# Hybrid RWKV-7 / forgetting-attention / MoE layer on one core: the forget gate in five pieces, one sum of squares a unit later, and the norms' chains in other places of the order

## The reference

```python
# forget gate of the attention
log_f = jax.nn.log_sigmoid(fl + f_bias)              # fl: 8 columns of u
c = jnp.transpose(jnp.cumsum(log_f, axis=1), (0, 2, 1))
s = jnp.einsum('bqhd,bkhd->bhqk', qb, k) + cb[..., :, None] - c[..., None, :]
...
o = o * lax.rsqrt(jnp.mean(o * o, axis=-1, keepdims=True) + RMS_EPS)   # norm of each head
# RWKV: the normalised kk, and the norm of y
kk = kk / jnp.maximum(jnp.sqrt(jnp.sum(kk * kk, axis=-1, keepdims=True)), 1e-12)
mean = jnp.mean(y, axis=-1, keepdims=True)
var = jnp.mean(jnp.square(y - mean), axis=-1, keepdims=True)
y = ((y - mean) * lax.rsqrt(var + RWKV_GN_EPS)).reshape(B, T, RWKV_WIDTH) * ln_w + ln_b
bonus = jnp.sum(r * k * r_k, axis=-1, keepdims=True) * v
return (y + bonus.reshape(B, T, RWKV_WIDTH)) * g
```

## Time and profile before

| | |
|---|---|
| median of 3 runs | 1685.38 us (1681.61 to 1690.52) |
| the profiled execution, its own time | 1686.94 us |
| its span | 1685.1 us |
| TensorE busy | 1606.7 us (95%) |
| VectorE busy | 1333.5 us (79%) |
| ScalarE busy | 1029.3 us (61%) |
| GpSimd busy | 605.2 us (36%) |
| granted TensorE clock, mean | 0.977 of full speed |

### The profile page before, as it was taken

How to read it: one execution, slowest core, us unless ns; L and a number is a source line. 1 busy time by engine, 2 the same in 40 slices (tenths; PEclk the granted TensorE clock), 3 DMA queues, 4 the chain that set the end, 5 groups by cost and what they waited for, 6 DMA issues and landing times.

```text
span 1685.1 us, 23225 instructions
## 1 busy us (share of the span) xinstructions
PE 1606.7 (95%) x7860; PEld 1166.6 (69%) x7860; DVE 1333.5 (79%) x1172; ACT 1029.3 (61%) x890; POOL 605.2 (36%) x398
## 2 busy tenths in 40 slices
PE   6999999989998999999999999999999999999993
PEld 5677877878566767777777777777777777777772
DVE  4479765434268989999899998999989999989893
ACT  4345235322155767777777777777777777777772
POOL 5633520232343213334344334343343432334320
PEclk9999979999998999999999999999999999999997
DMA  5322110201249999999999999999999999999994
GB/s 175 97 76 73 37 15 1 101 1 51 64 181 370 324 385 373 381 376 373 373 380 381 375 378 360 381 383 372 380 377 371 380 380 374 380 367 383 382 344 132
DMA packets 146543, 467.08 MB, mean 277 GB/s; under 512 B 21015, under 2 KB 35005, under 8 KB 146429
## 3 DMA queue, kind: packets, MB, share of 16 engines
q1 hardware_dynamic: 136684, 437.36, 69.0%
q0 software_dynamic: 9664, 28.53, 7.2%
q10 hardware_dynamic: 144, 0.52, 0.1%
HBM read 443.67 MB, written 22.71 MB: 277 GB/s over the span
## 4 chain that ended last, share of the span: by engine, by line
PE 82%; DVE 7%; DMA 5%; issue 2%; ACT 2%; POOL 1%; SPq 0%; DVEq 0%; POOLq 0%; ACTq 0%
PE banks L1638 20%; PE banks L1640 20%; PE banks L1639 20%; PE banks L1583 2%; PE banks L1312 2%; PE banks L1313 2%; PE banks L1314 2%; DMA slots<-in_expert_w_dram 2%; PE banks L1647 2%; PE banks L1633 1%; PE banks L1667 1%; PE banks L1489 1%; PE banks L1479 1%; PE banks L1376 1%; PE banks L1508 1%
## 5 line engine op out<-in xcount | busy, mean ns | idle before, releaser
L1963 DVE TENSOR_TENSOR lo<-slots,hi 128x2048 fp32r<-128x2048 f32 x384 | 863.0, 2286 | 55.9 <-PE banks L1640 49.1
L1107 ACT CAST hi<-slots 128x2048 fp32r<-128x2048 f32 x384 | 734.0, 1912 | 246.4 <-PE banks L1640 139.2
L1638 PE MATMUL banks<-lo,x_hi 128*96 128x512 f32 x1024 | 407.6, 398 | 0.0
L1640 PE MATMUL banks<-hi,x_lo 128*96 128x512 f32 x1024 | 403.8, 394 | 0.0
L1639 PE MATMUL banks<-hi,x_hi 128*96 128x512 f32 x1024 | 402.7, 393 | 0.0
L903 POOL DMA_INDIRECT x_sum<-hT,idy x32 | 91.1, 2848 | 468.3 <-ACT hT L1190 454.5
L928 POOL COPY idx_all<-ovf_pair 96x2 int32 x28 | 160.8, 5744 | 156.8 <-DMA ovf_pair<-slot_tokens,ovf_col 156.8
L1640 PEld LDWEIGHTS banks<-hi,x_lo 128*96 128x96 f32 x1024 | 165.7, 162 | 72.0
L1639 PEld LDWEIGHTS banks<-hi,x_hi 128*96 128x96 f32 x1024 | 166.3, 162 | 67.6
L1638 PEld LDWEIGHTS banks<-lo,x_hi 128*96 128x96 f32 x1024 | 166.0, 162 | 66.8 <-issue 0.2
L1638 PE MATMUL banks<-lo,a_hi 128*96 128x512 f32 x512 | 202.9, 396 | 6.0 <-DVE a_lo L2146 4.1
(11 more groups left out here) (369 smaller groups left out, 1964.2 us busy)
## 6 DMA issues: line engine op xcount, KB each, us to landing
slots<-in_expert_w_dram SPq DMA_DIRECT2D x384, 1024.0 KB, 10.2
slots<-in_w_in_dram SPq DMA_DIRECT2D x13, 1024.0 KB, 5.2
xs<-in_x_dram SPq DMA_DIRECT2D x8, 512.0 KB, 5.8
slots<-in_w_out_dram SPq DMA_DIRECT2D x2, 2048.0 KB, 7.8
x_sum<-xs SPq DMA_DIRECT2D x4, 512.0 KB, 9.4
h_rows<-slots SPq DMA_DIRECT2D x4, 512.0 KB, 3.4
xs<-x_sum SPq DMA_DIRECT2D x4, 512.0 KB, 7.1
x_sum<-xs POOLq DMA_DIRECT2D x3, 512.0 KB, 10.3
```

The lines of the kernel that those rows point to most:

```text
L1107: nc.scalar.copy(w_hi[n % HI][:, :, :], raw[r]).then_inc(hi_ready, 1)
L1638: nc.tensor.matmul(out, x_h, w_l, start=first, stop=False)
L1640: return nc.tensor.matmul(out, x_l, w_h, start=False, stop=last)
L1963: tensor_tensor(w_lo[n % LO][:, :, :], raw[n % RAW], w_hi[n % HI][:, :, :], ALU.subtract).then_inc(lo_ready, 1)
```

## The change

1. **Forget gate in pieces.** The scratch rows `fz` move to another slot (free until later), DVE still takes `fz[0]` behind the mix of unit 0, but ACT makes Abs and Exp behind unit 1 and Ln behind unit 2, and DVE does the rest behind the mix of unit 4 (`FF_BEHIND`). ACT no longer waits for `c3_ready` before the sigmoids but before the exponentials behind unit 8.
2. **Sum of squares.** The last of the four (j = 3) moves on PE behind unit 16, its root on ACT behind unit 18, its taking on DVE to the second elementwise chain. Unit 16 and this sum swap their places in the rotation of banks.
3. **Attention's norm.** The root moves from step i % 8 == 1 to 2, the multiplication to 3, the transposes to 5; two steps are added at the end; the first scores stand behind the first two KAR stages instead of ahead of them.
4. **y's norm.** For chunks 0 and 1 the root (ACT) stands behind kt of the next chunk, the reciprocal (DVE) and POOL's six steps behind its first KAR stage. The place of yT on PE stays.

```diff
-        fz = [region(slot_flat[3], (4 + n) * T, T)[0:H, :] for n in range(3)]
+        fz = [region(slot_flat[2], (1 + n) * T, T)[0:H, :] for n in range(3)]
...
+        FF_BEHIND = 4
...
-                for j in range(JT):
+                for j in range(JT - 1):
                     rot(("ss", j))
+            if m == 16:
+                rot(("ss", JT - 1))
...
-        FOX_STEPS = len(units) + 4
+        FOX_STEPS = len(units) + 6
...
-        rwkv_stages = [fox_stages[0]] + [("KAR", 0, g, 0) for g in range(2)] + [fox_stages[1]] \
-            + [("KAR", 0, g, 1) for g in range(2)] + [fox_stages[2]] + [("BR", 0, g) for g in range(2)] \
-            + [fox_stages[3]] + [("vt", 0), ("bt", 0)]
+        rwkv_stages = [("KAR", 0, g, 0) for g in range(2)] + [fox_stages[0]] + [("KAR", 0, g, 1) for g in range(2)] \
+            + [fox_stages[1]] + [("BR", 0, g) for g in range(2)] + [fox_stages[2]] + [("vt", 0), ("bt", 0)] + [fox_stages[3]]
...
-                if kind == "yT":
...
+                if kind == "yT" and tt >= 2:
+                    scale_y(tt)
+                if st in (("KAR", 1, 0, 0), ("KAR", 2, 0, 0)):
+                    scale_y(tt - 1)
...
-                if m == 0:
-
+                if m == 1:
                     emptied(act, "ff")
                     step(nc.scalar.activation(fz[1], fz[0], ACT.Abs))
                     step(nc.scalar.activation(fz[1], fz[1], ACT.Exp, scale=-1.0))
+                if m == 2:
                     nc.scalar.activation(fz[1], fz[1], ACT.Ln, bias=1.0).then_inc(ffln_ready, 1)
                 if m == 3:
                     act.wait_ge(consts_ready, 3)
-                    act.wait_ge(c3_ready, 1)
...
+                    act.wait_ge(c3_ready, 1)
                     act.wait_ge(cum_ready, j + 1)
...
+                if m == 18:
+                    act.wait_ge(kksum_ready, JT)
+                    nc.scalar.activation(AR[:, JT - 1, :, 0:C], AR[:, JT - 1, :, 0:C], ACT.Sqrt).then_inc(kknorm_ready, 1)
...
-                if i > H and i % H == 1:
+                if i > H and i % H == 2:
                     fox_rms(act, i // H - 1)
-                if i > H and i % H == 3:
+                if i > H and i % H == 5:
                     fox_out_T(act, i // H - 1)
...
+                    if kind == "kt" and tt in (1, 2):
+                        y_deviation(tt - 1)
...
+                if m == 16:
+                    square_sums(JT - 1)
...
-                if i > H and i % H == 3:
+                if i > H and i % H == 5:
                     fo_transposes(i // H - 1)
...
+                if m == FF_BEHIND:
                     step(tensor_scalar(fz[2], fz[0], 0.0, None, ALU.min))
                     dve.wait_ge(ffln_ready, 1)
...
+                if j == 1:
+                    take_squares(JT - 1)
                 dve.wait_ge(kknorm_ready, j + 1)
...
+                if i > H and i % H == 3:
+                    scale_fox(i // H - 1)
...
+                    if st in (("KAR", 1, 0, 0), ("KAR", 2, 0, 0)):
+                        y_scale(tt - 1)
...
-                    dve.wait_ge(gn_std_ready, tt + 1)
-                    nc.vector.reciprocal(var, var).then_inc(gn_rstd_ready, 1)
+                    if tt >= 2:
+                        y_scale(tt)
```

More of the change, by code:

```diff
@@ L525, in hymba_layer @@
                     put(("PT", *units[tt - 1]), 2)
-                if tt >= H + 3 and tt % H == 3:
+                if tt > H and tt % H == 5:
                     put(("foT", tt // H - 1), 2)
@@ L831, in _, with scale_y, heads @@
             nc.gpsimd.memset(XT.rearrange("p q f h t -> p (f q h t)"), 0.0).then_inc(xt_cleared, 1)
+            def scale_y(tt):
+                def heads(ap):
+                    return ap.rearrange("p (h v) -> p h v", h=H)
+                pool.wait_ge(gn_rstd_ready, tt + 1)
+                emptied(pool, "vt", tt)
+                for j in range(JT):
+                    emptied(pool, "bonus", j)
+                emptied(pool, "g", tt)
+                step(nc.gpsimd.tensor_tensor(heads(Yc), heads(Yc), gst[:, 1, :].unsqueeze(2).to_broadcast([P, H, N]), ALU.mult))
+                step(nc.gpsimd.tensor_tensor(heads(Yq), heads(V[tt % 2]),
+                                             bonus[:, tt, :].unsqueeze(2).to_broadcast([P, H, N]), ALU.mult))
+                step(nc.gpsimd.tensor_tensor(Yc, Yc, lnw[:, :], ALU.mult))
+                step(nc.gpsimd.tensor_tensor(Yq, Yq, lnb[:, :], ALU.add))
+                step(nc.gpsimd.tensor_tensor(Yc, Yc, Yq, ALU.add))
+                nc.gpsimd.tensor_tensor(Yq, Yc, G[:, tt, :], ALU.mult).then_inc(y_ready, 1)
             for j in range(JT):
@@ L1333, in bonus_products, with square_sums @@
                 end(ins, "bonus", j)
+            def square_sums(j):
+                ps = begin("ss", j)
+                pe.wait_ge(kksq_ready, j + 1)
+                end(nc.tensor.matmul(ps[:, :], blk[:, :], AR[:, j, :, 0:C], start=True, stop=True), "ss", j)
             for i, m in enumerate(U_ORDER):
@@ L1354, in _ @@
                         end(nc.tensor.matmul(ps[:, :], gl[:, tt * P:(tt + 1) * P], gup, start=True, stop=True), "g", tt)
-                    for j in range(JT):
-                        ps = begin("ss", j)
-                        pe.wait_ge(kksq_ready, j + 1)
-                        end(nc.tensor.matmul(ps[:, :], blk[:, :], AR[:, j, :, 0:C], start=True, stop=True), "ss", j)
+                    for j in range(JT - 1):
+                        square_sums(j)
+                if m == 16:
+                    square_sums(JT - 1)
                 if m > 22:
@@ L1845, in mix, with take_squares @@
                 dve.wait_ge(mixed, nth + 1)
+            def take_squares(j):
+                filled(dve, "ss", j)
+                tensor_scalar(AR[:, j, :, 0:C], chunks_of(bank[plan[("ss", j)][0]][:, :]), 1e-24, None, ALU.max)\
+                    .then_inc(free_of(("ss", j)), 1)
+                emptied(dve, "ss", j)
+                dve.sem_inc(kksum_ready, 1)
             rwkv_order = [m for m in U_ORDER if m < 14]
@@ L1869, in _ @@
                 if m == 11:
-                    for j in range(JT):
-                        filled(dve, "ss", j)
-                        tensor_scalar(AR[:, j, :, 0:C], chunks_of(bank[plan[("ss", j)][0]][:, :]), 1e-24, None, ALU.max)\
-                            .then_inc(free_of(("ss", j)), 1)
-                        emptied(dve, "ss", j)
-                        dve.sem_inc(kksum_ready, 1)
+                    for j in range(JT - 1):
+                        take_squares(j)
                 if m < 4 or m > 7:
```

31 lines of the change are left out of this document (12 added, 19 removed).

## The result

The changed kernel takes 1672.89 us (median of 7 runs, 1667.90 to 1675.22), the kernel before 1685.41 (7 runs, 1681.61 to 1690.52): a ratio of 0.9918, 95% interval 0.9902 to 0.9934, some 14 us less by the ratio and 12.5 by the medians. The forecast was 1667.4 in a range of 1658 to 1680; the gain was to be 18. The profiled execution took 1672.59 us, its span is 1670.8.

The account below looks back on a forecast made before the run. TensorE, busy 95% of the span, bounds the kernel; only its earlier start or full clock counts. Terms 1 + 2.3 + 2.2 + 12.5 = 18.0 us off the 1685.38 median give 1667.4 us, range 1658 to 1680.

Parts of the forecast that it names:

- y of chunks 0 and 1: RWKV chunks: waits of 6.24, 1.31 and 2.27 us go, plus 2.7 us of clock; 12.5 us won.
- Forget gate and sum of squares: Projection: TensorE gets 7 us sooner but waits for VectorE's chain; unit 16 and the total gain 1 us.
- The gate may meet one low part more than it did: 3.3 us later: VectorE's gate behind unit 4's mix: one more GpSimd low part met, scans of unit 4 3.3 us later.
- The fewer meetings in the bodies: VectorE's bodies of units 4 to 7: of six GpSimd low parts met, four counted now; 4 us back.
- TensorE's 7 us: Projection: what TensorE gains at the gate is spent waiting, 6 to 8 us idle ahead of unit 16.
- Attention and its end: Attention: 2.3 us from query-block ends and smaller waits; its end: 2.2 us from a shorter last-norm wait and clock.
- the forecast's second term: End of the attention: wait of 2.68 us shrinks to about 1.5, most half clock behind it goes; 2.2 us.
- rival (b): Waits return behind those removed, in the RWKV stage; half of y's and all the attention's gain lost: 1677, chance 0.17.
- the two small terms: Projection (gate and sum of squares), 1 us, and attention with its end, 2.3 + 2.2 us.
- (a): Projection: TensorE keeps the gate's 7 us because VectorE's chain isn't what unit 16 waits for; 1661, chance 0.09.
- (c): y stage: GpSimd again ends behind yT, so at most 5 us are won; 1680 to 1685, chance 0.07.
- (d): Attention: the clock stays at half, 17 to 34 us of work added; slower, up to 1701, chance 0.04.

Follow-up runs that it names:

- gate alone: The kernel before with only the forget gate in five pieces and its scratch rows, sums of squares as before: 1688.14 us (12 runs), ratio 1.0008.
- the gate one mix sooner: The changed kernel with the rest of the gate behind VectorE's third mix instead of the fourth (FF_BEHIND = 3): 1665.81 us (5 runs), ratio 0.9876.
- blocks first: The changed kernel with SyncE's last eight block writes ahead of the reads of the inverses, the read of blocks behind those: 1667.81 us, ratio 0.9883.

## Why the prediction was right, and where it was not

**y of chunks 0 and 1, 12.5 us: right.** Alone it gives 13.4 us by the medians and 14.3 by the ratio (interval 11.3 to 17.4), and 12.7 us in its trace. The mechanism is the one given: with GpSimd's steps put back, the wait of 6.24 us comes back as 6.22. The waits of 1.31 and 2.27 us are gone, and the clock is 1.00 from 340 to 380. This term carries the whole result.

**Forget gate and sum of squares, 1 us: not found, more likely a loss.** Alone the part costs 1.9 us by its ratio (0 to 3.9). The step that failed is "The gate may meet one low part more than it did: 3.3 us later": the scans of unit 4 start 4.6 us later (102.54 against 97.95). The count was right. The gate met one low part before, by this row of VectorE's timeline of the kernel before, and meets two now, 2.1 us each:

```profile
69.54 2.98 DVE L1861 TENSOR_TENSOR_SCAN slots<-slots 8x512 f32<-8x512 f32 x1
```

But the mix of unit 4 starts 6.1 us sooner and not 7 (88.62 against 94.70), and the gate behind it takes 10.7 us and not 10.3. The fewer meetings in the bodies came as forecast, four instead of six, 4.2 us back: VectorE's first mix behind them starts at 134.02, 0.35 us later than before, and unit 16 at 139.72, 0.2 us sooner instead of 1. The 1.1 us that the attention starts sooner in the first pair of traces was chance: the table has six traces with the old gate, 204.65 to 208.58 with a mean of 206.1, and six with the changed one, 206.44 to 207.89, mean 207.1. That TensorE's 7 us would be spent waiting was right in size (6.10), but it waits at unit 11, not ahead of unit 16: ScalarE's copy of unit 8 waits there for one of VectorE's mixes (it starts at 119.15), a table load, four exponentials and the cast for unit 11 (123.14) stand behind it, and GpSimd's low part (124.25) behind the cast. That the move of the last sum of squares is worth nothing held within what the runs can tell.

**Attention and its end, 2.3 + 2.2 us: most of it in the traces, not settled in time.** Alone they give 2.2 us by the ratio (0.5 more to 4.9 less). In the table the attention lasts 109.8 us on average over the five traces without these edits, and 107.8 over the six with them and the old order on SyncE: 2.1 us. Up to U of chunk 0, past the half clock that the forecast's second term counts, it is 117.7 against 114.0: 3.7 of the 4.5. The end went as I said and better: the wait of 2.68 is 0.29 to 0.30, where I left 1.5, and from the last transposes to U of chunk 0 it takes 6.2 instead of 7.6 to 7.9 us, about the 1.6 that I gave the clock there. What is missing lies in the attention itself. TensorE waits 1.75 to 2.9 us behind X0 in all six traces with these edits. In four of them VectorE stands 2.00 to 3.8 us for the blocks; in the other two it stands 0.54 and 0.62, and TensorE's wait of 1.75 comes a step later, behind rows of the inversion that take over 1 us instead of 0.2 while GpSimd masks. And the wait of 1.3 us that stays at the end of a query block has half clock behind it in five of these six traces, where 1.5 us of gain was put down with the clock in it. I first took the wait for the blocks as a thing that my edits brought. The kernel before has it too in its second trace (1.96 us), and with full clock up to X0 VectorE reaches the inversion 11.1 us behind the start with the edits and 10.3 us with the gate alone, so they don't bring it there sooner. It is rival (b)'s kind, a wait that a sooner engine runs into, but not its place (the chunks) nor its price. It hangs on SyncE's queue, which I did not follow.

**The sum.** In ratios: projection +1.9, attention -2.2, y -14.3 makes -14.6 us; the whole change measured -13.8 in its first set and -16.4 in the second. The parts add up within their intervals. Against the forecast the two small terms are 5.2 us short and y is 1.8 over; the 2 us that are left between that and 5.5 (1672.9 instead of 1667.4) are within the intervals. That the first pair of traces showed 17.6 us up to 385 us is no proof of the small terms: two executions of the kernel before differ by 2.8 us at the start of the attention. Theory and trace agreed there by luck, and the time lies in the stated range because y carries it.

**The other rivals.** (a), TensorE keeping the gate's 7 us, did not come; with the gate one mix sooner 5 us of them do: 202.01 at the start of the attention against a mean of 207.1. (c) and (d) left no sign; the clock from 208 to 236 is 0.76 as before.

Open: what VectorE's copy of the counts waits for, why two traces of the same kernel reach the attention 2.8 us apart (1.0 us at the wait for the low part, 71.59 and 70.56, and the first has two waits of 0.24 and 0.88 us behind it that the second hasn't; the half clock falls in other places), and whether the projection's edits are worth anything once the blocks come in time.

## What to carry to other kernels

When a step is moved so that an engine gets on sooner, look at the next thing that this engine will wait for, transfers above all, and follow it back through the queue of the engine that issues it: a transfer that is ready can stand behind one that is not. Put a side chain into the idle time of its engine, not behind it, and away from GpSimd's long instructions: by the medians one line of order was worth 5 us here, and another, on the DMA queue, 3. Before a wait is put down to the change, look for it in a second trace of the kernel before. And a term of 1 or 2 us can't be read from one pair of traces when two traces of the same kernel differ by more; read it from the same stage in several kernels that share that code.

## What was unexpected of the hardware

Two executions of one kernel show half clock in other places and of other length: 0.80 and 0.73 from 200 to 250 us with the same instructions, and even their waits differ (2.22 us at 241.16 in the one, 1.96 us at 222.51 in the other).

The same short wait had half clock behind it in one trace and not in the other. The wait of 1.3 us at the end of a query block is in all nine traces with the attention's edits; in four of them the clock stays at 1.00 behind it (243.97 in the changed kernel), in five it is half for some 7 us. TensorE alone from 244 to 248 us, the changed kernel and then the same kernel again (its wait is at 242.27):

```profile
244.00:248.00 4.00, 3.77 (x29) 1.00 0.00 0
```

```profile
244.00:248.00 4.00, 4.00 (x18) 0.50 0.00 0
```

One of 0.79 us at 212.14 in the changed kernel stood at the start of half clock, and the same wait, 0.80 us at 212.97 with blocks first, did not.

An attention without half clock took 101.2 and 101.4 us. With the gate sooner as well it took 105.0, all of the 3.8 us ahead of X0 (14.6 instead of 10.7), where the clock was 0.51 for 14 us; from there on the three agree within 0.1 us. So short waits can cost more in clock than in time, but a single trace doesn't tell which ones do.
